# Loading and multiplying a fourth modulation unit among the first projections, in place of one behind the router

## The reference, cut to what matters

```python
for l in range(DEPTH):                       # DEPTH = 2
    h = h + hybrid_mixer(rmsnorm(h, norm_mix[l]), w_in[l], ...)
    h = h + expert_choice_ffn(rmsnorm(h, norm_ffn[l]), w_router[l],
                              w_expert_gate[l], w_expert_up[l], w_expert_down[l])

def adaln(cvec, w, b):                       # of the second block, which runs after the layers
    m = jax.nn.silu(cvec) @ w + b            # w: 1024 x 6144
    return [t[..., None, :] for t in jnp.split(m, 6, axis=-1)]
sh1, sc1, gt1, sh2, sc2, gt2 = adaln(c, ada_w[l], ada_b[l])
csh1, csc1, ... = adaln(c_ctx, ada_w[l], ada_b[l])
```

## Time and profile before

| | |
|---|---|
| median of three executions | 2126.09 us |
| the profiled execution, its own time | 2128.85 us |
| its span in the profile | 2126.7 us |
| PE busy | 1916.9 us (90%) |
| DMA, bytes and mean rate | 748.18 MB, 352 GB/s |
| chain that ended last, by engine | PE 58%, DMA 36%, DVE 3%, ACT 2%, issue 1% |
| modulation units, line 1307 | 768 matmuls in both layers, twelve units |
| their loads | 12 of 2048 KB, median 18.3 us from issue to landing |

### The profile page before, as it was taken

The page is one execution under the profiler, slowest core; times in us unless marked ns, Lnnn a source line. Parts: engine busy times, 40 slices in busy tenths (PEclk is TensorE's granted clock), DMA queues, the critical chain, the costliest instruction groups (busy, mean ns, idle before and its releaser), DMA issues.

```text
span 2126.7 us, 31527 instructions
## 1 busy us (share of the span) xinstructions
PE 1916.9 (90%) x13966; PEld 1172.9 (55%) x13966; DVE 641.6 (30%) x988; ACT 553.7 (26%) x868; POOL 0.2 (0%) x4
## 2 busy tenths in 40 slices
PE   9999998787878999998898989889999998888887
PEld 8988832121312898883333434359999744434443
DVE  4576500000000558641331111037667300000001
ACT  4466300000000447620201222033544111111102
POOL 0000000000000000000000000000000000000000
PEclk9999999999999999999999999999999899999999
DMA  9735999999999962699999999974426999999997
GB/s 358 266 129 178 398 426 428 428 427 427 428 428 417 369 234 95 219 398 421 426 423 418 421 424 422 428 308 158 160 80 229 411 425 428 429 428 428 426 429 296
DMA packets 123007, 748.18 MB, mean 352 GB/s; under 512 B 6288, under 2 KB 27152, under 8 KB 83344
## 3 DMA queue, kind: packets, MB, share of 16 engines
q1 hardware_dynamic: 122896, 746.52, 86.1%
HBM read 745.45 MB, written 1.05 MB: 351 GB/s over the span
## 4 chain that ended last, share of the span: by engine, by line
PE 58%; DMA 36%; DVE 3%; ACT 2%; issue 1%; SPq 0%; DVEq 0%; ACTq 0%
PE bank L874 13%; DMA ring<-w_expert_up 12%; PE bank L965 10%; PE bank L1018 9%; DMA ring<-w_expert_down 9%; DMA arena<-moe_w_up 6%; PE bank L877 5%; DMA ring<-moe_w_up 5%; DMA ring<-w_expert_gate 4%; PE bank_pair L815 4%; PE bank_pair L818 2%; PE bank L996 2%; PE bank L901 1%; PE bank L1185 1%; PE bank L835 1%; PE bank L1206 1%
## 5 line engine op out<-in xcount | busy, mean ns | idle before, releaser
L965 PE MATMUL bank<-ring,arena 128*32 128x512 f32 (+1 forms) x3232 | 518.8, 507 | 93.2 <-DMA ring<-w_expert_up 38.9
L965 PEld LDWEIGHTS bank<-ring,arena 128*32 128x32 f32 x3232 | 166.1, 109 | 416.3 <-issue 211.9
L1018 PE MATMUL bank<-ring,arena 128*32 128x512 f32 x1280 | 282.7, 618 | 44.3 <-DMA ring<-w_expert_down 36.4
L1018 PEld LDWEIGHTS bank<-ring,arena 128*32 128x32 f32 x1280 | 69.9, 113 | 237.3 <-issue 179.0
L1871 ACT ACTIVATE arena<-bank 128x512 f32<-128x512 f32 (+1 forms) x130 | 66.8, 541 | 453.8 <-PE bank L980 216.8
L2447 DVE TENSOR_TENSOR arena<-arena,bank 128x512 f32<-128x512 f32 x24 | 15.8, 685 | 552.2 <-PE bank L965 552.2
L874 PE MATMUL bank<-extra_parts,ring_parts 128*128 128x256 f32 x1024 | 170.0, 283 | 0.0
L874 PEld LDWEIGHTS bank<-extra_parts,ring_parts 128*128 128x128 f32 x1024 | 140.4, 188 | 6.7 <-ACT arena_parts L1871 2.7
L874 PE MATMUL bank<-ring_parts 128*128 128x256 f32 x672 | 127.8, 284 | 2.1 <-DVE ring_parts L2874 1.1
L815 PE MATMUL bank_pair<-extra_parts,arena_parts 128*128 128x512 f32 x320 | 109.7, 396 | 0.0
L874 PEld LDWEIGHTS bank<-ring_parts 128*128 128x128 f32 x672 | 105.9, 189 | 3.7 <-DVE ring_parts L2874 1.3
(11 more groups left out here) (385 smaller groups left out, 2357.4 us busy)
## 6 DMA issues: line engine op xcount, KB each, us to landing
ring<-w_expert_down SPq DMA_DIRECT2D x62, 2048.0 KB, 23.9
ring<-w_expert_gate SPq DMA_DIRECT2D x58, 2048.0 KB, 22.5
ring<-w_expert_up SPq DMA_DIRECT2D x54, 2048.0 KB, 25.6
ring<-w_in SPq DMA_DIRECT2D x32, 2048.0 KB, 13.2
ring<-moe_w_up SPq DMA_DIRECT2D x24, 2048.0 KB, 27.6
ring<-moe_w_gate SPq DMA_DIRECT2D x20, 2048.0 KB, 39.8
arena<-moe_w_down SPq DMA_DIRECT2D x16, 2048.0 KB, 38.5
ring<-ada_w SPq DMA_DIRECT2D x12, 2048.0 KB, 18.3
```

The source lines that it names most:

```text
L965: last = pe.matmul(to[own_rows(half, e)].rearrange("p (q c) -> p q c", c=own), x_slots[:, c, 32 * e:32 * e + 32], w[:, k, half], start=c = ...
L1018: last = pe.matmul(banks[4 + e // PAIRS][own_rows(half, e), :].rearrange("p (x d) -> p x d", x=2), hidT[:, e // PAIRS * own + f % own, own ...
```

## The change

In `HEAD_ORDER` unit 21 (ada 3) moves from position 21 to position 10, between units 6 and 7. The units 7 to 17 move back by one position and so by one ring slot. Four units instead of three are multiplied early, the fourth ahead of unit 7; the copy of the results by ScalarE moves behind job 13. Two units instead of three stay behind the router. In the first expert tile unit 5 instead of unit 4 is loaded in halves, and unit 3 is issued ahead of unit 9.

```diff
-FIRST_LOADS = (2, 9, 3, 4, 5, 6, 7)
+FIRST_LOADS = (2, 3, 9, 4, 5, 6, 7)
...
-HEAD_ORDER = [0, 18, 1, 19, 2, 20, 3] + list(range(4, 18)) + [21, 22, 23]
+HEAD_ORDER = [0, 18, 1, 19, 2, 20, 3, 4, 5, 6, 21] + list(range(7, 18)) + [22, 23]
 HEAD_AT = {unit: p for p, unit in enumerate(HEAD_ORDER)}
-ADA_HEAD = 3
-ADA_WITH = ({1: (0,), 2: (1,), 3: (2,)}, {0: (0,), 1: (1,), 2: (2,)})
+ADA_HEAD = 4
+ADA_WITH = ({1: (0,), 2: (1,), 3: (2,), 7: (3,)}, {0: (0,), 1: (1,), 2: (2,), 7: (3,)})
...
-EARLY_ROWS = 4
+EARLY_ROWS = 5
...
-                ada_cols("ada 2", to_dve("ada 2 cols"), ada_rows, ADA_HEAD)
+                ada_cols("ada 3", to_dve("ada 3 cols"), ada_rows, ADA_HEAD)
...
-                    act.wait_ge(pe_done, pe_at(GATE_JOBS[n - GATE_BUFS][2] if n >= GATE_BUFS else "unit 6", loops))
+                    act.wait_ge(pe_done, pe_at(GATE_JOBS[n - GATE_BUFS][2] if n >= GATE_BUFS else f"unit {HEAD_ORDER[HEAD_AT[12] - RING]}", loops))
...
-                    if i == 7:
+                    if i == 13:
                         ada_copy(0, ADA_HEAD)
...
-                ada_cols("ada 2", bank_v(), ada_raw[:, kept:kept + 4 * ADA_HEAD, :])
+                ada_cols("ada 3", bank_v(), ada_raw[:, kept:kept + 4 * ADA_HEAD, :])
```

## The result

The changed kernel takes 2135.32 us (median of seven executions, 2133.94 to 2139.03), the kernel before, timed beside it, 2126.09 us (2123.58 to 2129.5). The ratio is 1.0042, 95% interval 1.0032 to 1.0051: slower by 9.2 us, where 3.9 us were forecast and the range ended at +6.9 us. The profiled execution took 2134.78 us with a span of 2132.7 us, so the two profiles are 6.0 us apart. The rest of the 9.2 us is that the profiled execution of before was itself 2.8 us over its median, and that of after 0.5 us under its own.

A forecast was written before the change was run, and what follows sets the result against it. Each layer's expert tiles were taken to end with their weight stream. Loads +1.2 and clock +0.75 gave +1.95 us a layer, +3.9 together: 2130.0 us for the median (2132.8 for an execution like the profiled one); range 2124.5 to 2133.0.

The forecast's parts named there:

- The unit in the head: Modulation unit inserted between jobs 12 and 13, on TensorE's chain: everything behind it 1.88 us later in each layer.
- The unit taken away: Behind the router, one of two units goes; VectorE's search releases the wait, so nothing gained, idle 1.18 to 3.06 us.
- No wait on unit 7's load: In the head, unit 7 lands at 73.9, ScalarE first reads it at 88.57: 14.7 us of cover, no cost.
- Unit 7 of the tile lands early: First expert tile: the load of unit 7 lands at 267.8 instead of 270.8, 3 us earlier.
- the queue then runs dry: First expert tile, ahead of unit 11: queue dry for 4.3 us because slots come free by TensorE's later work.
- The stream is 1.2 us later and stays so to the layer's end: Expert tiles: unit 12 lands at 281.9 against 280.65; term between -0.2 and +1.2 us a layer, +1.2 taken.
- the fourth rival: TensorE's longer path passed on in full, 3.8 us: 2129.9, or 2131.4; chance 0.32 shared with the full clock price.
- I take half, +0.75 us a layer: Line 901 and tile unit 0, behind the longer pause: TensorE's clock likely falls to half, costing +0.75 us a layer.
- full price: Clock fall over line 901 and tile unit 0: 1.5 us a layer, from a modulation unit's 3.36 instead of 1.88 us.
- I use 9.3 us: First expert tile: time from issue to landing of a lone 2 MB load; puts unit 11's landing at 277.0.
- the other end: Lone 2 MB load takes 7.9 us, as in the head: unit 11 lands at 275.6, term -0.2 us.
- the stream's rival: First expert tile: a lone load lands about 7 us after issue, unit 11 1.1 us early; -2.2 us, 2123.9; chance 0.10.

The follow-up runs named there:

- b_head: The kernel before with 8 idle 128-column calls ahead of job 13 in each layer: 2133.51 us against 2127.25, ratio 1.0034, +7.2 us.
- a_load: The changed kernel with one eighth of ada 3's products in the head and ada 4 behind the turned `aff`: 2126.89 us against 2126.83 for the kernel before, ratio 0.9996.
- b_gap: The kernel before with ada 4 cut to one of eight row blocks, lengthening the pause ahead of line 1463: 2131.28 us against 2127.25, ratio 1.0018, +3.8 us.

## Why the prediction was wrong

**Right.** The unit in the head costs 1.89 us. The unit taken away saves nothing on the path, because the search releases line 1463; the pause is 2.94 us. No wait on unit 7's load: ScalarE's split of it waits for TensorE after as before. Unit 7 of the tile lands early (264.8, forecast 267.8, before 270.8), and the queue then runs dry between 265 and 275 us.

**The step that failed: "The stream is 1.2 us later and stays so to the layer's end".** It took 1.88 us of lateness on TensorE and passed on only what unit 11's landing showed, as if behind it a full stream ran on. In the profile TensorE was 4.2 us late at the end of tile unit 0 (1.4 us of head, 2.8 us at the lower clock). Unit 11 landed at 277.5, 1.7 us later than before; then the spacing was 6.4, 5.6 and 4.9 us instead of 4.9 each, since each following load is also issued only when a tile unit frees its slot (269.97, 274.62, 279.26) and a queue with one or two loads in it moved 365 GB/s and not 427. Unit 12 is 3.3 us late, units 13 and 14 3.9 us, and the tiles pass on the whole 4.2 us of tile unit 0 but 0.3 us. The same holds in every kernel run: from the end of tile unit 0 to the next head it is 429.1 to 430.4 us, whether unit 11 lands at 272.7 or at 277.5; in the second layer, to the second block, 458.2 to 461.3 us. This was the fourth rival, the path passed on in full, which I said time alone could not tell from the forecast; its 3.8 us for two layers are still less than b_head's 7.2. Its reason, that the stream is not what ends the tiles, is not shown: unit 14 came 3.9 us late and the next head began 3.9 us late, so the stream may well end them. It then ran late by nearly the whole delay of TensorE, and not by 1.2 us. As for the moved load, a_load says it gives back at most 0.8 us a layer.

**The clock, "I take half, +0.75 us a layer".** Its full price was put at 1.5 us. Measured: line 901 +1.7 and tile unit 0 +1.0 us in the first layer, line 901 +1.5 us in the second, and +3.8 us for both with b_gap, timed. Over both layers of all profiles a pause of 2.0 us or more ahead of line 1463 was followed by the lower clock on line 901 in nine of ten cases, one of 0.2 to 1.2 us in one of thirteen, and none at all in one of seven. So the earlier trace rows, one fall in two pauses, was too small a sample, and the price is all that stands in the low stretch and not one unit's worth. The Trainium skill ("TensorE: Matmul & The Clock Gate", section "Why this matters for your kernels") asks for no long idle gaps between bursts; the trace agrees that the pause is followed by the lower clock, and b_gap puts its cost at about 2 us a layer.

**A lone load, "I use 9.3 us".** It took 7.3 to 7.5 us, below even the 7.9 us of the other end. The 9.4 us of unit 5 held about 2 us of queue: it was issued at 251.70, and the load ahead of it landed at 254.2. By the stream's rival this would have given a gain; it gave none, since unit 11 was itself issued at 269.97 and not at 267.69, and what stands behind it is released by TensorE. The Trainium skill's fixed cost ("DMA: Bandwidth & Descriptors", section "Anatomy of one DMA — SWDGE (gpsimd) path") of about 2.0 us, which the page gives for loads issued by GpSimd, is nearer to these rows than I allowed: 7.3 us less 4.85 us for the bytes leaves 2.5 us.

**Not seen at all: clock lost elsewhere.** In the second layer the low stretch began on the router's last products and added 1.3 us there. The window of the kernel after:

```profile
940.00:947.00 7.00, 7.00 (x100) 5.82 (x103) 1.34 (x6) 1.67 (x6) 0.00 (x0) 0.53 0.76 287
```

Before, only the unit of 3.35 us at 934.36 ran in one behind this router. Over 13 timed executions of the changed kernel the mean granted clock is 0.985, against 0.9877 before; by the slope above that is 1.7 us, part of it behind the long pause. I looked at one pause and took the rest of the run for unchanged.

**The account.** Head alone +7.2 and pause alone +3.8 make 11.0 us, less up to 1 us for the moved load (a_load timed: -0.9 us, interval -2.8 to +1.3), against 8.9 and 8.5 us measured in the two sets of runs, by the same reckoning; the intervals of the two parts (each some 2.4 us either way) cover the difference. In the profile it is 3.7 us of path, 5.6 us of clock behind the router in two layers, -0.9 us in the tiles. Open is why a later TensorE in the head loses clock in the second block: twice the calls brought about twice the excess (6.2 us over the path against 3.5), in five executions, but whether the delay does it or the added products themselves no kernel parts, and the profiles show only where the low stretches lie.

## What to carry to other kernels

Before moving work out of a stretch, look at who releases the wait behind it: here it was another engine's search, so the work taken away bought a pause, and the pause cost clock on what followed. Bytes moved out of a stretch were worth little here, where the slots, not the rate, held the next loads. And don't take a longer path to cost only its length: here two cost nearly twice as much, and a lower mean granted clock of the timed executions went with it, which two profiles can't show.

## What the runs showed of the hardware

- One execution of the same kernel differs from the next mostly by where the clock falls: of 94 executions of before the 16 with a mean granted clock of 0.990 or more have a median of 2125.1 us, the 15 with 0.985 or less 2130.1 us.
- The lower clock also came while TensorE was busy: 13.3 of 14 us in the window of before from 1661 to 1675 us, granted clock 0.52.
- A 2 MB load issued into an empty or nearly empty queue landed 7.3 to 7.5 us later, and the loads behind it 5.6 to 6.4 us apart, until the spacing was the 4.9 us of the full stream again.
- Ten idle products held the clock at the place they were put (line 901 at 2.02 us in both layers), and no gain was seen in the timed executions (+7.9 us, against +8.9 and +8.5 without them).
